# Later mean matmuls, four moved convolution taps and spread normalisations in a two-layer decoder trunk

## What is computed

```python
def odd_layer(x, g_norm, w_pw1, w_dw, b_dw, g_conv, w_pw2):
    z = rms_norm(x, g_norm) @ w_pw1
    y = z[..., :D_MODEL] * jax.nn.sigmoid(z[..., D_MODEL:])
    y = causal_depthwise_conv(y, w_dw, width=31) + b_dw
    return x + jax.nn.silu(rms_norm(y, g_conv)) @ w_pw2

def channel_mixer(x, g_norm, w1, w2):
    return x + jnp.square(jax.nn.relu(rms_norm(x, g_norm) @ w1)) @ w2
```

## Time and profile before

| what | value |
|---|---|
| median of 3 runs | 2119.3 us (2119.23 to 2120.34) |
| the profiled execution: its time, its span | 2119.95 us, 2118.2 us |
| PE busy | 2077.0 us, 98% |
| DVE busy | 1500.3 us, 71% |
| ACT busy | 924.4 us, 44% |
| POOL busy | 1019.8 us, 48% |
| granted TensorE clock | 0.998 |

### The profile page before, as it was taken

The page is one execution under the profiler, slowest core; times in us unless marked ns, Lnnn a source line. Parts: engine busy times, 40 slices in busy tenths (PEclk is TensorE's granted clock), DMA queues, the critical chain, the costliest instruction groups (busy, mean ns, idle before and its releaser), DMA issues.

```text
span 2118.2 us, 29952 instructions
## 1 busy us (share of the span) xinstructions
PE 2077.0 (98%) x9786; PEld 1736.7 (82%) x9786; DVE 1500.3 (71%) x2185; ACT 924.4 (44%) x1372; POOL 1019.8 (48%) x634
## 2 busy tenths in 40 slices
PE   7999899999999999999999999999999999999999
PEld 6788787888888898888888888887888888888887
DVE  6697658988888446378777667889863521779877
ACT  6554564332322664333323346435354323463562
POOL 6865753654655004556546557849775645000000
PEclk9999999999999999999999999999999999999999
DMA  5321112323333012323233223324333423433433
GB/s 216 97 65 59 71 41 63 117 90 100 100 91 100 10 53 80 100 80 113 96 99 100 90 90 90 109 81 140 99 90 100 140 90 119 139 120 110 138 129 120
DMA packets 69313, 208.30 MB, mean 98 GB/s; under 512 B 6976, under 2 KB 7232, under 8 KB 68928
## 3 DMA queue, kind: packets, MB, share of 16 engines
q1 hardware_dynamic: 69040, 206.57, 30.1%
q10 hardware_dynamic: 144, 0.02, 0.0%
HBM read 200.28 MB, written 6.29 MB: 98 GB/s over the span
## 4 chain that ended last, share of the span: by engine, by line
PE 85%; DVE 4%; POOL 4%; issue 3%; ACT 2%; DMA 0%; DVEq 0%; ACTq 0%; POOLq 0%; SPq 0%
PE psum L846 21%; PE psum L848 21%; PE psum L847 21%; PE psum L1172 5%; PE psum L1173 5%; PE psum L1174 5%; PE psum L1022 3%; PE psum L871 2%; POOL w_buf L1198 1%; PE psum L998 1%; PE psum L999 1%; DMA raw<-weights 0%; PE psum L929 0%; POOL hid_buf L1198 0%; PE psum L939 0%
## 5 line engine op out<-in xcount | busy, mean ns | idle before, releaser
L1198 POOL TENSOR_TENSOR w_buf<-raw,w_buf 128x1024 fp32r<-128x1024 f32 x270 | 660.8, 2448 | 455.4 <-ACT w_buf L1528 444.4
L846 PE MATMUL psum<-hid_buf,w_buf 128*128 128x512 f32 x1088 | 424.5, 390 | 1.7 <-DVE xt L2241 1.4
L848 PE MATMUL psum<-hid_buf,w_buf 128*128 128x512 f32 x1088 | 423.5, 389 | 0.0
L847 PE MATMUL psum<-hid_buf,w_buf 128*128 128x512 f32 x1088 | 423.5, 389 | 0.0
L1528 ACT ACTIVATE w_buf<-raw 128x1024 fp32r<-128x1024 f32 x256 | 269.5, 1054 | 339.9 <-PE psum L848 279.4
L846 PE MATMUL psum<-h_buf,w_buf 128*128 128x512 f32 x960 | 373.7, 389 | 2.2 <-POOL h_buf L1343 2.2
L847 PE MATMUL psum<-h_buf,w_buf 128*128 128x512 f32 x960 | 373.5, 389 | 0.0
L848 PE MATMUL psum<-h_buf,w_buf 128*128 128x512 f32 x960 | 373.5, 389 | 0.0
L2264 DVE SCALAR_TENSOR_TENSOR psum<-y_buf,wdw,psum 128x512 f32<-128x512 f32 x435 | 295.0, 749 | 0.0
L846 PEld LDWEIGHTS psum<-hid_buf,w_buf 128*128 128x128 f32 x1088 | 204.3, 188 | 44.7 <-issue 1.8
L848 PEld LDWEIGHTS psum<-hid_buf,w_buf 128*128 128x128 f32 x1088 | 204.3, 188 | 42.5
(11 more groups left out here) (327 smaller groups left out, 3091.9 us busy)
## 6 DMA issues: line engine op xcount, KB each, us to landing
raw<-weights SPq DMA_DIRECT2D x320, 512.0 KB, 3.5
w_more<-weights SPq DMA_DIRECT2D x36, 512.0 KB, 4.2
xt<-x_t SPq DMA_DIRECT2D x2, 2048.0 KB, 8.6
out_t<-xt SPq DMA_DIRECT2D x16, 256.0 KB, 2.0
x_in<-x_t SPq DMA_DIRECT2D x12, 256.0 KB, 7.1
early<-weights SPq DMA_DIRECT2D x4, 512.0 KB, 7.8
x_kept<-xt SPq DMA_DIRECT2D x1, 2048.0 KB, 8.6
h_first<-x_kept SPq DMA_DIRECT2D x1, 2048.0 KB, 9.6
```

Of the source, the lines that this page charges most:

```text
L846: nc.tensor.matmul(acc, lhs_hi, rhs_hi, start=first, stop=False)
L847: nc.tensor.matmul(acc, lhs_hi, rhs_lo, start=False, stop=False)
L848: return nc.tensor.matmul(acc, lhs_lo, rhs_hi, start=False, stop=last)
L1198: nc.gpsimd.tensor_tensor(dst_lo, src, dst_hi.bitcast(F32), ALU.subtract).then_inc(done, 1)
```

## The change

`mean_of` is called behind `k == 4` of unit 1 in place of `k == 1`: nine matmuls later, at all eight means. `FF1_TAPS` has five taps in place of six after the first four units of ff1/0; the four taps that are left go behind unit 4 of the second chunk, which had one and has five. The copy to `rms_kept` moves from the end of ff1/0's root to the start of its second chunk. `normalise_inputs`, sixteen DVE instructions in one piece behind the eighth up unit of ff1/1, becomes one instruction behind each of the eight up units (`normalise_second`) and one behind each of the eight down units (`normalise_first`).

```diff
-FF1_TAPS = [6] * 16
+FF1_TAPS = [5] * 4 + [6] * 12
...
-                    if k == 1 and mean:
+                    if k == 4 and mean:
                         mean_of(*mean)
...
-            def normalise_inputs():
-
-                dve.wait_ge(h_second_up, KT)
-                for k in range(KT):
-                    V.tensor_tensor(h_second[:, k, :], h_second[:, k, :], rms_bc[:], ALU.mult).then_inc(h_second_up, 1)
-                dve.wait_ge(h_first_in, 16)
-                for k in range(KT):
-                    V.scalar_tensor_tensor(out=h_first[:, k, :], in0=h_first[:, k, :], scalar=gflat(G_FF1, k),
-                                           in1=rms_kept[:], op0=ALU.mult, op1=ALU.mult).then_inc(h_first_up, 1)
+            def normalise_second(i, r):
+                k = 4 * i + r
+                V.tensor_tensor(flat(h_second, None, k), flat(h_second, None, k), rms_bc[:], ALU.mult
+                                ).then_inc(h_second_up, 1)
+
+            def normalise_first(i, r):
+                k = 4 * i + r
+                V.scalar_tensor_tensor(out=flat(h_first, None, k), in0=flat(h_first, None, k), scalar=gflat(G_FF1, k),
+                                       in1=rms_kept[:], op0=ALU.mult, op1=ALU.mult).then_inc(h_first_up, 1)
...
-                if (stage, half) == ("ff1", 0):
-                    link(V.tensor_copy(rms_kept[:], rms_bc[:]))
...
                     if late:
+                        link(V.tensor_copy(rms_kept[:], rms_bc[:]))
                         squares = conv_squares(1)
...
+                    elif (stage, half) == ("ff1", 1) and q == 0:
+                        dve.wait_ge(h_second_up, KT)
+                        units(up, 8, relu_scaled, normalise_second)
+                        dve.wait_ge(h_first_in, 16)
                     else:
                         units(up, 8, relu_scaled, more_topk(0))
-                    if (stage, half) == ("ff1", 1) and q == 0:
-                        normalise_inputs()
...
                     else:
-                        units(down, 8, add_residual(down, half), more_topk(1))
+                        first_inputs = normalise_first if (stage, half) == ("ff1", 1) else None
+                        units(down, 8, add_residual(down, half), more_topk(1), first_inputs)
```

## The result

The changed kernel takes 2124.0 us (median of 22 executions, 2122.6 to 2128.2), the kernel before 2119.3 us (22 executions, 2117.1 to 2122.0): ratio 1.0023, 95% interval 1.0017 to 1.0029. It is slower, by 4.7 us. Forecast was 2120.8, with 2123.4 as the upper end of the range. The profiled execution took 2123.59 us, its span is 2121.9.

The account below looks back on a forecast made before the run. PE, busy 1756.5 of 1768.0 us behind 350 us, bounds the kernel. Terms 0.6 - 0.6 - 0.4 + 0.2 - 0.5 + 2.6 - 0.4 = +1.5 us on 2119.3 gave 2120.8 us, 80% between 2116.8 and 2123.4.

Parts of the forecast that it names:

- unit 4's waits from L1198: Brackets of 0.1 to 1 at unit 4's first matmul in ff0/0, ff0/1, conv0, pw1/1, conv1 and ff1/1.
- ff0/0 +0.6: In ff0/0 the mean comes 0.59 us later on the clock and DVE has no slack: +0.6 us.
- In ff1/0, up to the first down unit's start: Taps and copy in ff1/0: POOL ends the pause at 1462.75 earlier, -0.5 us, bounds 0 and -1.8.
- The sum of squares behind unit 4 meets the split: ff1/0's second chunk: four moved taps make the sum wait for POOL's split, +2.6 us up to conv1's unit 5.
- waits that simply go: Rival: jobs behind the mean have slack, so mean, burst and taps gain 7.7 us, 2111.6 us; 6%.
- four hidden taps: Rival: ff1/0's second-chunk taps find idle DVE time; total about -1 us, 2118.3 us; 22%.
- the sums of units 5 to 7 did not snowball: Rival, end of ff1/0's second chunk: each sum waits for a split, adding 5.7 us, 2126.5 us; 7%.
- the spread normalisations alone cost nothing: Rival in ff1/1: normalisations beside splits lengthen POOL and cost more than the burst, +2 us, 2122.8 us; 10%.
- the bound of 11.5 us: Behind 350 us, all stages together can give back at most 11.5 us of PE time, 0.5% of the kernel.
- PE is busy ... at full granted clock: Behind 350 us PE is busy 1756.5 of 1768.0 us at full granted clock; the case is only about PE pauses.
- the -0.4 for ff1/1: In ff1/1: -1.5 us for the burst's pause, +1.1 us for unit 4's wait and longer split, together -0.4 us.
- the burst's pause of 1.52 goes: In ff1/1, spreading the sixteen normalisations removes PE's pause behind DVE's burst, 1.52 us.

Follow-up runs that it names:

- load behind ten: Changed kernel with the load of h_first issued behind ten weight blocks of ff1/1 instead of eight: 2124.7 us, ratio 1.0029.
- taps only: Kernel before with only the four taps moved behind unit 4 of ff1/0's second chunk: 2120.35 us, ratio 1.0007.
- taps in down units: Kernel before with the four taps from ff1/0's first four units put behind its first four down units: 2118.3 us, ratio 0.9998.
- six later where free: Kernel before with the mean six matmuls later only in ff0/1, conv0 and pw1/1: 2116.5 us, ratio 0.9993.
- Normalisations alone: Kernel before with only the sixteen normalisations spread over the units of ff1/1: 2118.5 us, ratio 0.9998.
- ff1/1 only: Kernel before with the mean nine matmuls later in ff1/1 alone: 2121.0 us, ratio 1.0014.
- mean-only: Kernel before with only the eight means nine matmuls later, run twice: 2124.3 us (ratio 1.0026) and 2123.7 us (ratio 1.0023).
- old taps: Changed kernel with FF1_TAPS as in the kernel before: 2122.3 us, ratio 1.0015.
- ff1/0 as before: Kernel before with the mean nine matmuls later in all stages but ff1/0: 2121.5 us, ratio 1.0013.
- six later: Kernel before with the mean six matmuls later in all eight stages, nothing else changed: 2118.9 us, ratio 1.0005.
- with ff1/0: Kernel before with the mean six matmuls later in ff0/1, conv0, pw1/1 and also ff1/0: 2118.5 us, ratio 1.0001.
- combined: Kernel before with mean six later in ff0/1, conv0, pw1/1, four taps behind ff1/0's first down units, copy and normalisations as changed: 2115.7 us, ratio 0.9986.
- before with the load behind ten: Kernel before with the load of h_first behind ten weight blocks instead of eight: 2119.5 us, ratio 1.0002.

## Why the prediction was wrong

**What held.** No bracket at any L859; unit 4's waits from L1198 in five of the six places named (ff0/1 has 0.02 and starts 0.2 late). ff0/0 +0.6 (forecast +0.6), ff0/1 -0.5 (-0.6), conv0 -0.3 (-0.4), pw1/0 0 (0), pw1/1 +0.3 (+0.2). In ff1/0, up to the first down unit's start (1462.75, now 1462.23) -0.5 (-0.5), with 2.52 in the bracket where about 2.6 was named. The sum of squares behind unit 4 meets the split: from that down unit to the start of conv1's unit 5 (1574.25, now 1577.80) the changed trace takes 4.07 us more; without the clock's 1.6 that is about 2.4, forecast +2.6. The rivals of waits that simply go and of four hidden taps are out; the sums of units 5 to 7 did not snowball (1.54 to 2.79 us each, before 1.55 to 2.78), and the spread normalisations alone cost nothing (-0.3). Two small slips changed little: the bound of 11.5 us leaves out 1.07 us of the first mean's pause, which the 10.3 us of pauses hold, and the lower bounds that the prediction names add up to 2118.5, not 2118.8.

**What failed first: "PE is busy ... at full granted clock", taken over from the kernel before, so that the sum has no term for the clock.** It took each pause at its length, and the section ahead of it said that a gain can come only from idle times. The changed kernel has two pauses of 2.5 us: one because the wait at ff1/0's mean moved into the wait before its first down unit, one because the moved taps delay the end of the second chunk. Behind one of them its profile has the half clock, 1.6 us that no bracket shows. That gathering alone brings this is shown by the pair that differs in nothing but where ff1/0 waits. In both profiles with two such pauses (the changed kernel, and the same with the load behind ten) the clock fell behind one of the two; over all profiles it fell behind eleven of fourteen pauses of 2.0 to 2.9 us, by which the changed kernel would pay 2 x 11/14 x 1.6 = 2.5 us on average. So 1.6 to 2.5 us (estimate from these counts), and the kernel before about 0.5, with one such pause and one fall in three profiles. The mean clock of whole executions can't decide between them: at 0.998 they took 2122.6 to 2123.7 us and at 0.995 2128.2, but at 0.996 and 0.997 anything from 2123.4 to 2126.7, and the figure also holds half clock ahead of 350 us, which every kernel here has.

**What failed second: the -0.4 for ff1/1, by its first part, "the burst's pause of 1.52 goes".** The pause was in the profiled execution and in the earlier trace rows, but in neither of two others of the same kernel, nor in five more profiles in which ff1/1 and its burst are untouched (taps only, taps in down units, the three with six later where free): one of eight in all. Normalisations alone gain 0.3, not 1.5. Against the usual execution the changed kernel's ff1/1 is +1.6 (0.08 + 1.5): 0.9 at unit 4, 0.5 at the first down unit (brackets 0.74 and 0.32, and 0.16 each), 0.2 unplaced. Without that pause in its base the forecast for ff1/1 would have been +1.1. The late mean brings the burst's pause about: all six profiles with a later mean in ff1/1 and the burst in one piece have it (0.84 to 1.62), and ff1/1 only costs +1.8. The spreading takes it away again (mean-only to old taps: +5.5 and +5.2 to +3.5, of which the ff1/0 column gives about 0.4 to the copy), so the edit earns in this company what it does not earn alone.

**The account.** Net of the table + 1.5 for the unusual pause, against the difference of the medians: changed kernel 3.8 + 1.5 = 5.3 (measured +4.7), with the load behind ten 5.5 (+5.9); old taps 3.9 (+3.5); mean-only 4.9 and 6.2 (+5.5, +5.2); taps only 2.1 (+1.5); normalisations only -0.2 (-0.3); mean in ff1/1 only 2.8 (+1.8); ff1/0 as before 2.1 (+2.3); six later 0.3 (+0.3), where free -2.1 (-2.1), with ff1/0 -0.4 (-0.3); taps in down units -0.8 (-0.2); combined -3.2 (-3.1). Most agree within 1 us; the worst is before with the load behind ten, 2.7 (+1.0), whose trace holds a fall. Of the 3.2 us between forecast (+1.5) and result (+4.7) ff1/1 has about 2.0 (+1.6 against -0.4) and the clock about 1.1 or more (1.6 in the profile, less the 0.5 that the kernel before pays on average). Beyond that single profiles do not resolve.

**What stays open.** What puts POOL a split behind at the start of ff1/1's burst with the late mean: not the place of the `h_first` load alone. That POOL's position decides is read from the rows of fifteen profiles; no run changed it alone. Also open is what makes the pause of 0.2 to 1.4 at ff1/1's first down unit, which four traces with the late mean have and others lack. And why the clock fell behind 2.04 and 2.10 us, but not behind 2.68 at 1462 in the changed kernel, 2.63 at 1554 and 2.01 at 1463 in two others. How often it falls in executions that were not profiled is not shown either.

## What to carry to other kernels

Moving a wait later on an engine that is 98% busy does not shorten it if what it waited for feeds a later wait: the pieces add up there, and one long pause can cost more than several short ones with the same sum, because the clock may fall behind it. So move a wait only in the stages where nothing waits for its result again, and leave waits apart in the others. Here nine matmuls later in all stages cost 5.5 us, six later in all 0.3, and six later in the three free stages alone gained 2.1. Before a pause that the profile shows is counted as a gain, see it in a second execution of the same kernel: 1.5 us of forecast hung on one that two other profiles of the kernel did not have.

## What the runs showed of the hardware

TensorE's granted clock went to half (start to start 0.43 us, the 1.2 GHz level) for 3.4 us, though PE was busy from the first slow matmul to the last. The first slow matmul was in one trace the one that ended the pause (1461.36, 0.80 us, waits gathered in ff1/0); in the ten others it started up to 1.6 us behind it. With a pause counted as its bracket + 0.16, the clock fell behind eleven of the fourteen between 2.0 and 2.9 us (brackets 1.85 to 2.76), and behind none of the eighteen between 1.4 and 1.95. The length alone does not decide: behind 2.04 it fell, behind 2.68 it did not. In the two profiles with two long pauses it fell behind one of them only, the second at 1552 once (full behind 2.68 at 1462), the first at 1463 the other time (full behind 2.63 at 1554). The stretch shows in no bracket and in no releaser; it shows as matmuls of 0.63 us instead of 0.39, or in a row of busy time by stretches.
